# Prompt attention on one core: queries turned straight from the projection's rows, the upper half of the query tile written twice by the scalar engine, the residue over 64 rows

## The reference, cut to what matters

```
qs = q * (HEAD_DIM ** -0.5)
p_c = masked_softmax(einsum('bqhgd,bchd->bqhgc', qs, kv_cmp[:, :, 0]), m_c)      # 16 compressed blocks
p_s = masked_softmax(einsum('bqhgd,bqhkd->bqhgk', qs, kv_sel[..., 0, :]), m_s)   # selected rows
p_w = masked_softmax(einsum('bqhgd,bkhd->bqhgk', qs, kv_band[:, :, 0]), m_w)     # a window of 512
return gates[..., 0:1] * o_c + gates[..., 1:2] * o_s + gates[..., 2:3] * o_w
```

## Time and profile before

| | us |
|---|---|
| median of 3 runs | 1014.05 |
| lowest, highest of them | 1013.36, 1018.79 |
| the profiled execution | 1020.7 |
| its span from first to last instruction | 1019.0 |
| PE busy | 935.7 (92%) |
| DVE busy | 595.0 (58%) |
| ACT busy | 409.7 (40%) |
| POOL busy | 190.9 (19%) |

### The profile page before, as it was taken

The page is one execution under the profiler, slowest core; times in us unless marked ns, Lnnn a source line. Parts: engine busy times, 40 slices in busy tenths (PEclk is TensorE's granted clock), DMA queues, the critical chain, the costliest instruction groups (busy, mean ns, idle before and its releaser), DMA issues. The chain is left out here.

```text
span 1019.0 us, 16705 instructions
## 1 busy us (share of the span) xinstructions
PE 935.7 (92%) x5935; PEld 808.9 (79%) x5935; DVE 595.0 (58%) x1428; ACT 409.7 (40%) x916; POOL 190.9 (19%) x178
## 2 busy tenths in 40 slices
PE   5999999998989988999999988999688999999997
PEld 5999999998979887777889867777445666777665
DVE  6531010194444576878555668787567867787653
ACT  6432111111023454666534445667264434434322
POOL 0049599999010000000000230000000000000000
PEclk9999999998999999999999979999688999999999
DMA  7127534534052101000011013300533455452321
GB/s 252 53 97 241 194 114 147 175 118 125 1 169 67 48 16 36 1 1 1 9 43 50 23 39 101 108 1 1 191 91 103 128 166 163 139 160 68 116 89 32
DMA packets 106820, 93.73 MB, mean 92 GB/s; under 512 B 21245, under 2 KB 99954, under 8 KB 104626
## 3 DMA queue, kind: packets, MB, share of 16 engines
q1 hardware_dynamic: 84946, 58.65, 19.1%
q10 hardware_dynamic: 19488, 17.25, 5.6%
q0 software_dynamic: 2304, 16.78, 4.8%
HBM read 78.16 MB, written 18.61 MB: 95 GB/s over the span
## 5 line engine op out<-in xcount | busy, mean ns | idle before, releaser
L592 PE MATMUL ps<-w_hi,h_hi 128*128 128x264 f32 (+5 forms) x432 | 123.9, 287 | 0.2 <-DVE h_lo L464 0.2
L592 PE MATMUL ps<-w_lo,h_hi 128*128 128x264 f32 (+5 forms) x432 | 122.9, 284 | 0.0
L592 PE MATMUL ps<-w_hi,h_lo 128*128 128x264 f32 (+5 forms) x432 | 122.8, 284 | 0.0
L1269 DVE TENSOR_TENSOR pt_lo<-ps,pt_hi 128x512 fp32r<-128x512 f32 x132 | 90.9, 689 | 52.0 <-ACT pt_hi L1190 51.4
L1190 ACT ACTIVATE pt_hi<-ps 128x512 fp32r<-128x512 f32 x132 | 78.6, 597 | 83.2 <-PE ps L1099 82.3
L472 DVE TENSOR_TENSOR w_lo<-w_raw,w_hi 128x1024 fp32r<-128x1024 f32 (+3 forms) x13 | 33.6, 2585 | 128.0 <-ACT w_hi L366 128.0
L1265 DVE TENSOR_REDUCE least<-ps 128x1 f32<-128x640 f32 (+7 forms) x128 | 90.0, 703 | 14.1 <-PE ps L1088 12.9
L313 POOL TENSOR_TENSOR chunk<-chunk 128x1024 f32<-128x1024 f32 (+2 forms) x46 | 82.5, 1793 | 3.6
L592 PEld LDWEIGHTS ps<-w_hi,h_hi 128*128 128x128 f32 (+1 forms) x432 | 79.6, 184 | 0.5 <-issue 0.4
L592 PEld LDWEIGHTS ps<-w_lo,h_hi 128*128 128x128 f32 (+1 forms) x432 | 79.6, 184 | 0.0
L592 PEld LDWEIGHTS ps<-w_hi,h_lo 128*128 128x128 f32 (+1 forms) x432 | 79.3, 184 | 0.0
(11 more groups left out here) (379 smaller groups left out, 2257.4 us busy)
## 6 DMA issues: line engine op xcount, KB each, us to landing
kv_pages<-in_cache_slc_kv SPq DMA_DIRECT2D x256, 64.0 KB, 1.9
shared<-in_x_prompt SPq DMA_DIRECT2D x8, 512.0 KB, 3.6
w_raw<-in_w_in SPq DMA_DIRECT2D x8, 512.0 KB, 3.9
wr_raw<-in_w_in SPq DMA_DIRECT2D x8, 512.0 KB, 4.0
kv_window<-in_cache_win_kv SPq DMA_DIRECT2D x4, 1024.0 KB, 5.8
wo_raw<-in_w_out SPq DMA_DIRECT2D x8, 512.0 KB, 9.0
out<-in_cache_win_kv SPq DMA_DIRECT2D x1, 4032.0 KB
x_row<-in_x_prompt ACTq DMA_DIRECT2D x7, 512.0 KB, 4.2
```

Source lines behind the costliest of these rows:

```text
L592: mm = nc.tensor.matmul(out, lhs, rhs, start=(k == 0 and i == 0), stop=(k == KD - 1 and i == 2))
L1269: nc.vector.tensor_tensor(pt_lo[:, t % PTS, :], ps[:, turn_bank(t), :], pt_hi[:, t % PTS, :].bitcast(F32), ALU.subtract).then_inc(s_ptl, 1)
```

## The change

The staging of the queries on DVE goes (tile, semaphore and both operations). PE turns 64 columns of `pq`, the projection's own rows, into the lower 64 partitions of the bank. ACT writes that to both halves of `q_hi`, with the scale, in two ACTIVATEs of 64x512. `q_lo` is made over the lower 64 rows only, by a SCALAR_TENSOR_TENSOR; its upper half is set to zero once, by POOL. The product q_lo * k_lo is no longer computed.

```diff
-        q_st = sb("q_st", [P, NG, 2, HD])
...
-        s_qst = sem("q_staged")
...
                 nc.gpsimd.memset(wv2[:, :], 0.0).then_inc(s_w2z, 1)
+                g.did(nc.gpsimd.memset(q_lo[:].bitcast(F32), 0.0))
...
                         if x % NT == 0:
                             pe.wait_ge(s_klo, 6 * (x // NT) + 6)
-                        pe.wait_ge(s_qst, x + 1)
                         out = spare(("q", x))
                         for g in range(NG):
-                            mm = nc.tensor.transpose(out[:, g * P:(g + 1) * P],
-                                                     q_st[:, g, :, :].rearrange("p a d -> p (a d)"), ident[:, :])
+                            c = (x // NT * NG + g) * HD
+                            mm = nc.tensor.transpose(out[0:HD, g * P:(g + 1) * P], pq[:, x % NT, c:c + HD], ident[:, :])
                         mm.then_inc(s_sp, 1)
...
                         act.wait_ge(s_sp, place["q", x] + 1)
-                        nc.scalar.activation(q_hi[:, x % 2, :], ps[:, 7, :], ACT.Copy).then_inc(s_qhi, 1)
+                        for rows in (slice(0, HD), slice(HD, P)):
+                            mm = nc.scalar.activation(q_hi[rows, x % 2, :], ps[0:HD, 7, :], ACT.Copy, scale=-SCALE)
+                        mm.then_inc(s_qhi, 1)
...
-                def stage_query(x):
-                    kv, i = x // NT, x % NT
-                    src = pq[:, i, kv * NG * HD:(kv + 1) * NG * HD].rearrange("p (g d) -> p g d", g=NG)
-                    nc.vector.tensor_scalar(q_st[:, :, 0, :], src, -SCALE, None, ALU.mult)
-                    nc.vector.tensor_scalar(q_st[:, :, 1, :], src, -SCALE, None, ALU.mult).then_inc(s_qst, 1)
...
-                    if what == "k_stage":
-                        if x == 0:
-                            stage_query(0)
-                    elif what == "v_stage":
+                    if what == "v_stage":
...
                         dve.wait_ge(s_qhi, x + 1)
-                        nc.vector.tensor_tensor(q_lo[:, x % 2, :], ps[:, 7, :],
-                                                q_hi[:, x % 2, :].bitcast(F32), ALU.subtract
-                                                ).then_inc(s_spr, 1)
-                        if x + 1 < NKV * NT:
-                            stage_query(x + 1)
+                        nc.vector.scalar_tensor_tensor(q_lo[0:HD, x % 2, :], ps[0:HD, 7, :], -SCALE,
+                                                       q_hi[0:HD, x % 2, :].bitcast(F32), ALU.mult, ALU.subtract
+                                                       ).then_inc(s_spr, 1)
```

## The result

| | before | after |
|---|---|---|
| median, us (lowest to highest, runs) | 1014.61 (1013.36 to 1018.79, 4) | 1027.07 (1024.25 to 1032.82, 4) |
| the profiled execution, us | 1020.7 | 1028.16 |
| mean granted clock of it | 0.958 | 0.956 |

The changed kernel is slower: the ratio is 1.0123, with a 95% interval of 1.0069 to 1.0176. The forecast was 1018.3 us, its range ended at 1023.5, and the result lies 3.6 us above it. Two more series of six runs on other chips gave 1.0105 [1.0060, 1.0149] and 1.0109 [1.0077, 1.0141], so this is no accident of one chip.

The account below looks back on a forecast made before the run. PE, busy 374.94 of the stage's 410 us, waits at query steps for the chain through ACT and DVE. 4.8 us lost there less 0.6 at the start gives +4.2 us on 1014.05: 1018.3 us, range 1011 to 1023.5.

Parts of the forecast that it names:

- DVE's slack is worth nothing while it waits for ACT: Query steps: work taken from DVE helps only where PE waits for DVE; DVE idles 17.8 us before q_lo for ACT.
- DVE paces the stage: Rival, attention stage: ACT's second write is hidden and DVE's saving reaches PE, 6.6 us faster, 1007.5 us; chance 0.12.
- `q_lo` at 0.69 us, four transposes at no gain: Query steps: q_lo over 64 rows still takes 0.69 us, and PE's 64-column transposes save zero.
- the 64-column loads pay: Rival, PE's query transposes: each takes half its place, and 4.2 us saved cancel the loss, 1014.1 us; chance 0.06.
- The second write adds 0.47 us: ACT's second q_hi write overlaps the first and lengthens the chain to c_scores by 0.47 us a step.
- no overlap: Alternative price of ACT's second q_hi write if the two do not overlap: 0.59 us, not taken.
- the losses at c_scores: PE at the 16 query steps: c_scores comes 0.47 us later, less any slack after q_lo.
- what was given back: Behind c_scores in steps 6, 7, 11 and 14: PE's later waits for exponentials shrink, absorbing part of the loss.
- The start of the stage gains 0.6 us: Start of the attention stage: without the first staging wr_lo and PE come 0.60 us earlier; POOL's extra memset is hidden.
- The clock: Rival: longer waits before c_scores bring more half-clock stretches on PE, 5 us more, +9.2 us, 1023.3 us; chance 0.20.
- step 7's wait of 0.87 us had no such end: Argument against more half-clock stretches: PE's 0.87 us wait before c_scores in query step 7 was not followed by one.

Follow-up runs that it names:

- e4: The changed kernel with POOL's memset of q_lo moved behind its other constants: 1026.54 us, ratio 1.0107.
- e12: The kernel before, with DVE's staging and one more TENSOR_SCALAR put between the wait for q_hi and q_lo (+0.60 us): 1024.05 us, ratio 1.0088.
- e2: The changed kernel, with DVE released after ACT's first q_hi write and the second write copying from SBUF: 1010.48 us, ratio 0.9955.
- e1: The kernel before, staging kept, with only ACT's q_hi write split into two of 64 rows: 1031.1 us, ratio 1.0161.
- e10: The kernel before, with DVE's staging of the next query moved between the wait for q_hi and q_lo (+0.40 us): 1016.06 us, ratio 1.0004.
- e9: The kernel before with the query step one head earlier, all else unchanged: 1005.56 us, ratio 0.9918.

## Why the prediction was wrong

1. *DVE's slack is worth nothing while it waits for ACT.* Right. `least` follows `q_lo` by 0.61 us in the 14 steps where it stands next, DVE's wait rose from 17.8 to 26.7 us (25 forecast), and the rival "DVE paces the stage" fell.
2. *`q_lo` at 0.69 us, four transposes at no gain.* Right: `q_lo` takes 0.68 us, and the transposes gained nothing. Both traces by source (the weight load, then the matmul), before and after:

```profile
L1056 PEld LDWEIGHTS ps<-ident,q_st x64: 138/141/224, 299.9 to 670.6; 128*128 128x128 f32 x64
```

```profile
L1055 PEld LDWEIGHTS ps<-ident,pq x64: 108/110/113, 297.5 to 676.0; 128*64 128x64 f32 x64
L1055 PE MATMUL ps<-ident,pq x64: 270/272/300, 297.6 to 676.1; 128*64 128x128 f32 x64
```

   The load is 31 ns shorter, so it does go with its columns as the rule of the Trainium skill ("TensorE: Matmul & The Clock Gate", section "LDWEIGHTS (loading the stationary operand)") that the prediction weighed says, though by less than the rule's 53 ns. The matmul is not shorter, and nothing of the 31 ns reaches the chain. That has to be read where ACT waits for PE, as in step 4 (timelines of PE and ACT, before and after); in step 7 ACT comes to `q_hi` straight from an exponential, and its delay tells nothing of PE.

```profile
382.13 0.63 PE L1056 MATMUL ps<-ident,q_st 128*128 128x128 f32 x4 [1.15 <-DVE scaled L1283]
...
382.79 0.60 ACT L1170 ACTIVATE q_hi<-ps 128x512 fp32r<-128x512 f32 x1 [2.01 <-PE ps L1056]
```

```profile
383.01 0.63 PE L1055 MATMUL ps<-ident,pq 128*64 128x128 f32 x4 [1.06 <-DVE scaled L1272]
...
383.67 1.19 ACT L1169 ACTIVATE q_hi<-ps 64x512 fp32r<-64x512 f32 x2 [1.92 <-PE ps L1055]
```

   From the first transpose to `q_hi` it is 0.66 us in both. The rival "the 64-column loads pay" fell.
3. *The second write adds 0.47 us.* Wrong by a quarter, the first mis-sized term of the sum. I read it off two ACTIVATEs that both covered 128 partitions. The chosen 0.47 should have been the 0.59 that stood beside it as "no overlap": 0.60 us was measured over the 16 steps. So the losses at c_scores were 7.4 us instead of 6.2, what was given back 1.8 instead of 1.4 us, and with 0.4 us gained at the query steps, which the forecast did not have, the sum 5.3 instead of 4.8 us. Steps and structure were right, and the later waits took the part that was forecast of them.
4. *The start of the stage gains 0.6 us.* Wrong, the second mis-sized term: nothing is left of it. PE's wait of 0.50 us became 0.41 us in one trace and 0.66 us in the two others. The step priced the removed staging and counted POOL's memset as hidden because POOL had time; it did not ask whom the memset disturbs. It stretched the DVE operation beside it by 0.5 to 0.75 us, and e4 shows that without it the gain appears.
5. *The clock.* The step that failed: the forecast put the clock's share at nothing. I set it up as a rival, with a chance of 0.20, 5 us and the total of 1023.3 us. In the runs it was the rule: the mean granted clock fell from 0.9643 to 0.957 and took some 5 us. The size was about right, the chance was not. The argument against it ("step 7's wait of 0.87 us had no such end") took one wait of one trace for evidence on fourteen that all become longer; by then the same trace had 34.1 us at half clock in the stage, of which the prediction looked at 6.9. It also added to a sum that was itself too low: 4.2 forecast, 6.1 measured at equal clock, and 5.1 on top. The 6.1 and the 5.3 to 5.5 outside half clock agree within the spread of the regression (4.9 to 6.5); segments at half clock, in which a wait may cost as well, are left out of the latter. The range ended where the clock's case did, at 1023.5 us, and that case stood on the low sum; this is most of why the result lies above it.

What is shown: the chain's length is the cause (e12 makes four fifths of the loss with none of the change's parts, e2 undoes it with all of them), and the second write makes the chain longer (e1). That the lower clock takes its 5 us is worked out from the spread of the runs and from the traces; no experiment changed the clock alone. What stays open: why the clock falls between +0.40 and +0.60 us, and which of the waits tips it. Other parts of the program that feed the same bank were not tried as covers.

## What to carry to other kernels

Price an added instruction by the chain it stands in, not by its engine's idle time: ACT was idle half the stage, and its second write still set PE back by 7 us. Read the price from a neighbouring pair of the same shape and the same partitions; where no such pair is in the trace, take the end without overlap. And where a matrix engine is over 90% busy and its clock is just short of full, give a wait that comes back each tile a second price through the clock: here it was 5.1 us on top of 6.1, and nothing in e10, whose waits were 4.2 us more than before; signalling the first half as soon as it is there (e2), or laying other work over the chain (e9), costs a few lines.

## What the runs showed of the hardware

- **A write to the upper 64 partitions overlaps neither of its neighbours on ACT.** Two of 64x512, one on 0:64 and one on 64:128, start 0.586/0.602/0.605 us apart (least, median, most of 16), and the next ACTIVATE, of 128 partitions, starts 0.024 us behind the end of the second. It holds whether the source shifts partitions (changed kernel) or not (e1). Where both writes begin at partition 0 the next starts 0.11 us before the end, also when one has 128 rows and the other 64. This is ACT ahead of step 3 in the changed kernel: 357.98 lies before 357.50 + 0.59.

```profile
357.50 0.59 ACT L1198 ACTIVATE oT<-ps 128x512 f32<-128x512 f32 x1
357.98 1.18 ACT L1169 ACTIVATE q_hi<-ps 64x512 fp32r<-64x512 f32 x2
```

  So it is not a different number of partitions that prevents the overlap; two writes in a row on 64:128 were not tried. The Trainium skill ("ScalarE: Activation LUTs", section "What ACT_TABLE_LOAD costs") says that ACTIVATEs back to back overlap by about 93 ns. This case agrees with that where both begin at partition 0 (0.11 us) and not around a write to 64:128.
- **A POOL memset stretches a DVE operation beside it.** A TENSOR_SCALAR of 128x192 took 0.594 us beside memsets of 0.32 and 0.21 us (before, e4), and 1.09 to 1.34 us beside one of 128x1024 that itself took 0.95 us. In all sixteen traces it ends 0.11 us behind the end of a memset, so it seems to wait for one; no trace has it without a memset beside it. The Trainium skill ("GPSIMD Engine Reference", section "1. Specifications") says that the engine's access to SBUF is shared with VectorE, with contention for DVE instructions in a 2-port mode or with two SBUF inputs. The trace agrees that there is contention, with these numbers; the instruction has one input, and no row tells its mode.
- **The mean clock does not follow the added wait in proportion.** With 8 waits of 5.3 us together (before) it was 0.9643, with 12 of 9.5 us (e10) 0.967, with 14 of 12.4 us, none over 1.5 us, in a stage of 440 us (changed kernel) 0.957.
